# A recurrence's projection and its preparation, put into one stage with the low rank tile first

## The reference

```
h = x @ w_in[l];  p = first 1664 columns of h
p = p + mu * (p_prev - p)                       # p_prev: p one position earlier
r, k, v, wl, al = split(p, 512, 512, 512, 64, 64)
w_log = -softplus(-(w0 + tanh(wl) @ w2)) - 0.5
decay = exp(-exp(w_log));  a = sigmoid(a0 + al @ a2)
kk = k * k_k, each head of 64 divided by its norm
k = k * (1 + (a - 1) * k_a)
step t:  S = S * decay + (S @ -kk) (kk * a)^T + v k^T;   y = S @ r
y = group norm of y + sum(r * k * r_k) * v
```

## Time and profile before

| | us |
|---|---|
| Median of 3 runs | 3826.53 |
| Lowest and highest of them | 3826.25, 3833.31 |
| The profiled execution, its device time | 3837.09 |
| Its span in the profile | 3835.3 |
| PE busy in it | 3369.2 |
| DVE busy | 1380.3 |
| ACT busy | 1086.7 |
| POOL busy | 1404.6 |

### The profile page before, as it was taken

The page is one execution under the profiler, slowest core; times in us unless marked ns, Lnnn a source line. Parts: engine busy times, 40 slices in busy tenths (PEclk is TensorE's granted clock), DMA queues, the critical chain, the costliest instruction groups (busy, mean ns, idle before and its releaser), DMA issues. The chain is left out here.

```text
span 3835.3 us, 52393 instructions
## 1 busy us (share of the span) xinstructions
PE 3369.2 (88%) x20950; PEld 2515.3 (66%) x20950; DVE 1380.3 (36%) x2308; ACT 1086.7 (28%) x1770; POOL 1404.6 (37%) x791
## 2 busy tenths in 40 slices
PE   6688899899967889997999697989999988789998
PEld 5474477566445764775665375678888866467786
DVE  2642463577425424453775322630000032340000
ACT  2313323312023233223211342532212233342221
POOL 4321434522024223344321114734324332655453
PEclk9899899999988999998999898999999989899999
DMA  3001032345210010232443210012111111012232
GB/s 113 7 4 55 29 115 72 121 172 190 88 57 31 3 40 22 94 110 72 186 165 137 76 34 33 9 53 66 61 66 61 62 52 45 23 61 88 85 102 83
DMA packets 75032, 282.17 MB, mean 74 GB/s; under 512 B 8320, under 2 KB 8320, under 8 KB 73888
## 3 DMA queue, kind: packets, MB, share of 16 engines
q1 hardware_dynamic: 74784, 278.76, 21.4%
HBM read 276.62 MB, written 2.10 MB: 73 GB/s over the span
## 5 line engine op out<-in xcount | busy, mean ns | idle before, releaser
L129 POOL TENSOR_TENSOR lows<-ring,highs 128x1024 fp32r<-128x1024 f32 x328 | 813.8, 2482 | 1733.2 <-ACT highs L121 1733.1
L150 PE MATMUL ps<-x_high,highs 128*128 128x512 f32 x2128 | 861.4, 405 | 138.8 <-POOL lows L129 105.7
L153 PE MATMUL ps<-x_low,highs 128*128 128x512 f32 x2128 | 840.1, 395 | 0.0
L154 PE MATMUL ps<-x_high,lows 128*128 128x512 f32 x2128 | 839.6, 395 | 0.0
L150 PEld LDWEIGHTS ps<-x_high,highs 128*128 128x128 f32 x2128 | 407.2, 191 | 240.5 <-POOL lows L129 121.1
L121 ACT ACTIVATE highs<-ring 128x1024 fp32r<-128x1024 f32 x328 | 346.7, 1058 | 714.0 <-PE ps L150 617.6
L153 PEld LDWEIGHTS ps<-x_low,highs 128*128 128x128 f32 x2128 | 407.6, 192 | 91.2 <-issue 9.3
L154 PEld LDWEIGHTS ps<-x_high,lows 128*128 128x128 f32 x2128 | 406.4, 191 | 87.3
L1405 DVE CUSTOM_DVE_ANT_0 X<-X 128x1024 f32<-128x1024 f32 x192 | 321.7, 1675 | 118.4 <-DMA X<-in_ada 112.4
L1361 PE MATMUL ps<-BR,ring 128*128 128x512 f32 x512 | 236.1, 614 | 27.6 <-POOL BR L1413 16.3
L2196 DVE TENSOR_TENSOR hidden_scratch<-ps,hidden_scratch 128x512 f32<-128x512 f32 x66 | 39.8, 603 | 557.2 <-PE ps L154 555.1
(11 more groups left out here) (359 smaller groups left out, 4965.5 us busy)
## 6 DMA issues: line engine op xcount, KB each, us to landing
ring<-in_w SPq DMA_DIRECT2D x402, 512.0 KB, 3.6
X<-in_ada SPq DMA_DIRECT2D x96, 512.0 KB, 6.6
more_tiles<-in_dft SPq DMA_DIRECT2D x2, 2048.0 KB, 8.3
X<-in_xT SPq DMA_DIRECT2D x4, 512.0 KB, 7.4
X<-in_memT SPq DMA_DIRECT2D x2, 1024.0 KB, 5.0
X<-in_cond SPq DMA_DIRECT2D x4, 512.0 KB, 5.5
out<-xT SPq DMA_DIRECT2D x1, 2048.0 KB, 6.3
cst<-in_cst SPq DMA_DIRECT2D x1, 1408.0 KB, 10.4
```

Source lines behind the costliest of these rows:

```text
L129: nc.gpsimd.tensor_tensor(self.low(n), self.chunk(n), self.high(n).bitcast(F32), ALU.subtract).then_inc(self.lo_made, 1)
L150: mm = nc.tensor.matmul(ps, high, xhigh, start=start, stop=False)
L153: nc.tensor.matmul(ps, high, xlow, start=False, stop=False)
L154: return nc.tensor.matmul(ps, low, xhigh, start=False, stop=stop)
```

## The change

The two stages become one. The chunks of w_in are stored in the order RW_ORDER = (12, 4, 5, 6, 7, 0, 1, 2, 3, 8, 9, 10, 11): low rank tile, k, r, v. Chunk i of this order is tile RW_ORDER[i] and goes to bank i % 4; banks 4 to 7 are for the preparation's matmuls. PE now waits for DVE's mix of chunk i-4 before it reuses the bank, since DVE reads the tile from PSUM as well.

SP sends the first chunk, the parameters, two more chunks, and only then clears the other pool. praw has two slots instead of 13, and the mix takes the unshifted tile from PSUM. The 32 operations that fill AR become 8, each over all 512 positions.

The steps of the preparation stand behind the work of chunk i on each engine:

| engine | behind chunk i |
|---|---|
| PE | 1: w2 products; 2: a2 products; 5: norm sums; 10: bonus sums |
| ACT | 0: tanh; 1 and 2: sigmoids; 3 and 5: decays (4 Exp each); 4: squares; 6: Ln; 7: Exp |
| DVE | 1 to 4: one k * k_k each; 2: scans; 3: k_a scale; 4: new k; 6: bound; 8: kk, kk * a; 9: r * k * r_k; 10 and 11: AR; end: bonus |
| POOL | low parts up to chunk 8, 9, 10, 11, each followed by one k product; chunk 12, then four kk * a products, then the next stage's first low part |

```diff
+RW_ORDER = (12, 4, 5, 6, 7, 0, 1, 2, 3, 8, 9, 10, 11)
...
             def _(sp):
+                stream.send(sp, n0 + 1)
+                sp.dma_start(par[:, :], A["par1"][bass.ds(layer, 1), :, :].rearrange("l p c -> p (l c)")).then_inc(S("par"), 16)
+                stream.send(sp, n0 + RING)
                 clear(sp, other)
+                stream.send(sp, n0 + RW_TILES + RING - 1)
+                sp.wait_ge(S("par"), 16)
...
             def _(pe):
+                for i in range(RW_TILES):
+                    if i >= 4:
+                        pe.wait_ge(S("mixed"), i - 3)
+                    gemm3(pe, i % 4, n0 + i, XH, XL, S("product"))
+                    if i == 1:
+                        pe.wait_ge(S("tanh"), 1)
+                        for c in range(4):
+                            nc.tensor.matmul(PS[:, 4 + c, :], w2a2[0:64, c * P:(c + 1) * P], TH[0:64, :], start=True, stop=True).then_inc(S("lora"), 1)
+                    if i == 2:
+                        for c in range(4):
+                            pe.wait_ge(S("gates"), c + 1)
+                            nc.tensor.matmul(PS[:, 4 + c, :], w2a2[64:128, c * P:(c + 1) * P], M[64:128, 12, :], start=True, stop=True).then_inc(S("lora"), 1)
+                    if i == 5:
+                        pe.wait_ge(S("gates"), 8)
+                        for c in range(4):
+                            pe.wait_ge(S("ksq"), c + 1)
+                            nc.tensor.matmul(PS[:, 4 + c, :], C("head_ones", P), TMP[:, c, :], start=True, stop=True).then_inc(S("knorm2"), 1)
+                    if i == 10:
+                        for c in range(4):
+                            pe.wait_ge(S("rkr"), c + 1)
+                            pe.wait_ge(S("kfloor"), c + 1)
+                            nc.tensor.matmul(PS[:, 4 + c, :], C("head_ones", P), TMP[:, c, :], start=True, stop=True).then_inc(S("bonus_sum"), 1)
...
+                for n, steps in ((8, ()), (9, (k_tilde, 0)), (10, (k_tilde, 1)), (11, (k_tilde, 2)), (12, (k_tilde, 3)), (13, (b_tilde, 0))):
+                    stream.lo(nc, pool, n0 + n)
+                    if steps:
+                        steps[0](steps[1])
+                for c in range(1, 4):
+                    b_tilde(c)
+                stream.lo(nc, pool, n0 + RW_TILES + 1)
...
+                    a.activation(praw[:, i % 2, 1:T + 1], PS[:, i % 4, :], ACT.Copy).then_inc(S("evicted"), 1)
+                    stream.hi(nc, act, n0 + min(i + 3, RW_TILES + 1))
...
+                for i, t in enumerate(RW_ORDER):
+                    dve.wait_ge(S("evicted"), i + 1)
+                    v.tensor_tensor(diff[:, i % 2, :], praw[:, i % 2, 0:T], PS[:, i % 4, :], ALU.subtract).then_inc(S("diff"), 1)
+                    dve.wait_ge(S("diff"), i + 1)
+                    v.scalar_tensor_tensor(out=M[:, t, :], in0=diff[:, i % 2, :], scalar=par_col("mu", t),
+                                           in1=PS[:, i % 4, :], op0=ALU.mult, op1=ALU.add).then_inc(S("mixed"), 1)
...
+                    if i == 8:
+                        for c in range(4):
+                            dve.wait_ge(S("kinv"), c + 1)
+                            v.tensor_tensor(KK[:, c, :], KK[:, c, :], SG[:, c, :], ALU.mult).then_inc(S("kk"), 1)
+                        for c in range(4):
+                            dve.wait_ge(S("kk"), c + 1)
+                            v.tensor_tensor(AA[:, c, :], AA[:, c, :], KK[:, c, :], ALU.mult).then_inc(S("b0"), 1)
+                    if i == 9:
+                        for c in range(4):
+                            dve.wait_ge(S("mixed"), 6 + c)
+                            dve.wait_ge(S("kmod"), c + 1)
+                            v.scalar_tensor_tensor(out=TMP[:, c, :], in0=M[:, c, :], scalar=par_col("r_k", c), in1=M[:, 4 + c, :],
+                                                   op0=ALU.mult, op1=ALU.mult).then_inc(S("rkr"), 1)
...
-    out = [cols("rw", t) for t in range(13)]
+    out = [cols("rw", t) for t in RW_ORDER]
```

More of the change, by code:

```diff
@@ L502, in first @@
         n0 = FIRST["rwkv"]
-        praw = X[:, 30 * T:30 * T + 13 * 513].rearrange("p (c t) -> p c t", c=13)
         M = XT(0, 13)
[L505 to L545, removed]
         SG, LC = XT(13, 4), XT(17, 4)
@@ L580, in _, with k_tilde @@
             @block.gpsimd
             def _(pool):
-                for c in range(4):
+                def k_tilde(c):
                     pool.wait_ge(S("decays"), 2 * c + 2)
@@ L585, in _, with b_tilde @@
                     nc.gpsimd.tensor_tensor(KT[:, c, :], M[:, 4 + c, :], PI[:, c, :], ALU.mult).then_inc(S("k_tilde"), 1)
+                def b_tilde(c):
                     pool.wait_ge(S("b0"), c + 1)
                     nc.gpsimd.tensor_tensor(BT[:, c, :], AA[:, c, :], PI[:, c, :], ALU.mult).then_inc(S("b_tilde"), 1)
+                for n, steps in ((8, ()), (9, (k_tilde, 0)), (10, (k_tilde, 1)), (11, (k_tilde, 2)), (12, (k_tilde, 3)), (13, (b_tilde, 0))):
[5 more added lines that the diff above has]
+                stream.lo(nc, pool, n0 + RW_TILES + 1)
             @block.scalar
@@ L591, in _ @@
                 a = nc.scalar
[L592 to L609, removed]
@@ L617, in _ @@
                 v = nc.vector
+                v.memset(praw[:, :, 0:1], 0.0).then_inc(S("zeroed"), 1)
                 v.memset(PP[:, :, :, 0:1], 1.0).then_inc(S("first_decay"), 1)
[L619 to L641, removed]
-                    v.scalar_tensor_tensor(out=TMP[:, c, :], in0=M[:, c, :], scalar=par_col("r_k", c), in1=M[:, 4 + c, :],
-                                           op0=ALU.mult, op1=ALU.mult).then_inc(S("rkr"), 1)
@@ L644, in _ @@
[L644 to L659 removed]
+                dve.wait_ge(S("par"), 16)
```

94 lines of the change are left out of this document (76 added, 18 removed).

## The result

The changed kernel takes 3794.4 us (median of 4 runs, 3793.7 to 3796.5), against 3829.9 (3826.3 to 3836.1, 4 runs) for the kernel before on the same chip: a recorded ratio of 0.9897, 95% interval 0.9879 to 0.9914 (the two medians alone give 0.9907). That is faster, by about 1%, but above the forecast of 3772.3 and above its range (3757 to 3788). The profiled execution took 3793.7 us with a span of 3791.9, against 3837.1 and 3835.3 before.

The account below looks back on a forecast made before the run. TensorE bounds most of the kernel, but waits in the preparation on a VectorE/ScalarE chain. Per layer 46.2 + 3.5 - 13.8 - 5.7 - 3.1 = 27.1 us, twice 54.2, from 3826.5 to 3772.3; range 3757 to 3788.

Parts of the forecast that it names:

- the stall at the bonus sums: After tile 10, PE waits 2.0 to 3.2 us per layer for VectorE's r * k * r_k products; taken 2.6.
- the scans: Behind chunk 2, four VectorE scans may hold out GpSimd's low part: PE stalls 0 to 0.9 us, taken 0.5.
- preparation removed: Between the last product and the scan's first matmul, the whole 46.2 us goes, in each of two layers.
- head: At the stage's opening, the first chunk goes out earlier: gain 3.5 us per layer, ends 2.7 and 3.9.
- matmuls among the tiles: Sixteen fp32 matmuls on PE between GEMM tiles, 0.86 us each at full clock: 13.8 us per layer.
- tail: After the last product, eviction, mix, bonus products and boundary remain: 5.7 us per layer, ends 4.9 and 8.
- rival 1: Smooth case: no stalls, short tail, scan opening at full clock; 32.7 us per layer, 3761; chance 0.18.
- ACT's slots: Behind chunks 3, 6 and 7, table load and four functions end by +5.1 or +5.2, under 5.44 us: no cost.
- Starved GpSimd: In the GEMM, closed VectorE bursts hold low parts to their end; PE loses 14 us per layer, 3794; chance 0.13.
- The third: In-order engines hold the added steps until the last tile; only 9.0 us per layer saved, 3809; chance 0.03.
- the fourth: Slower than before: late steps carry from tile to tile, 3 us stall in each, 3844; chance 0.03.
- the forecast's own: Main case across the stage: stalls of 1 to 6 us per layer, 3764 to 3783 us; chance 0.62.

Follow-up runs that it names:

- The run with the constants: Changed kernel plus five fp32 128x512 matmuls on constants on PE behind chunk 10, ahead of the wait for r * k * r_k: 3790.2 us, ratio 0.9880.
- both runs on it: Changed kernel with SyncE's old order (clear, parameters, chunks) put back: 3801.4 us. Kernel before with only the new order: 3831.7 us.
- The fills in place of the products: Changed kernel with GpSimd's eight k_tilde and b_tilde products replaced by memsets: 3788.2 us; the same replacement in the kernel before: 3823.2 us.

## Why the prediction was right or wrong

The direction held, and so did most of the mechanism; the stall at the bonus sums, which left out two causes, did not, and neither did the base. The miss of the median is 3794.4 - 3772.3 = 22.1 us. I split it first:

- 10.8 us: the sum was 54.2, and the profiled executions differ by 43.4. Of this 10.2 lie in the terms below and 0.6 outside the stage.
- 10.6 us: the base. I carried the sum from the profiled execution to a median of three runs that lay 10.6 us lower, as if that distance would stay. The changed kernel's median is within 1 us of its profiled execution. In three later sets of runs, on three chips, the kernel before had medians of 3837.7 (7 runs), 3838.4 (15) and 3834.5 (13), 8 to 12 above the 3826.5. So the three runs may be a low draw, or their chip may be a faster one; no run tells which.
- 0.7 us: the rest, the median of 3794.4 against the profiled 3793.7.

Either of the first two alone would have left the time inside the range (3772.3 + 10.8 = 3783.1).

The sum, term by term, for both layers. The forecast's stall term of 3.1 per layer is 0.5 for the scans and 2.6 for the bonus sums.

| term | forecast | measured | difference in gain |
|---|---|---|---|
| preparation removed | 92.4 | 92.3 | -0.1 |
| head | 7.0 | 7.8 | +0.8 |
| matmuls among the tiles | 27.6 | 29.3 | -1.7 |
| tail | 11.4 | 12.9 | -1.5 |
| stalls | 6.2 | 13.9 | -7.7 |

**The stall at the bonus sums** is the step that failed. The place (after tile 10), the engine that ends it and the operand were as forecast. The size was not: I had 2.0 to 3.2 us, and it was 6.4 and 7.5 beyond the sums' 3.44. Two things were wrong in it. First, I let VectorE's eight products meet GpSimd's low parts alone: one to wait for until +4.0 and one of 2.3 us in the row or behind it. The row took 11.2 us instead of 4.9, and the timelines of the changed kernel show four operations of GpSimd beside it, two low parts and two k products:

```profile
93.84 2.39 POOL L130 TENSOR_TENSOR lows<-ring,highs 128x1024 fp32r<-128x1024 f32 x1 [1.78 <-ACT highs L122]
94.23 5.45 DVE L656 TENSOR_TENSOR X<-X 128x512 f32<-128x512 f32 x4
96.19 1.74 POOL L556 TENSOR_TENSOR BR<-X 128x512 f32<-128x512 f32 x1
99.28 2.66 POOL L130 TENSOR_TENSOR lows<-ring,highs 128x1024 fp32r<-128x1024 f32 x1 [1.35 <-ACT highs L122]
99.60 5.77 DVE L659 TENSOR_TENSOR X<-X 128x512 f32<-128x512 f32 x4
101.90 1.72 POOL L556 TENSOR_TENSOR BR<-X 128x512 f32<-128x512 f32 x1
```

In my list of the slots GpSimd's k products had no place, although the change's table has one behind each of these low parts. Their part is shown by two experiments that take them away in different ways: both give a row of 9.0 us and a wait of PE of 2.24 us in both layers, 2.2 less. That is inside the 2.0 to 3.2 that I had, so the wait was priced rightly but for the k products. (The +9.9 of the working should read +8.9, 4.0 + 4.9; with the low part's 2.3, the mix's 1.5 and a first product of 0.7 that is 13.4, inside its 13 to 14, so the slip moved nothing.) That the low parts hold the rest follows from the rows, but no run took those away. Second, I priced the idle time at its length alone. PE left it at a lower clock, 0.65 over the sums of layer 0, and slot 10 was 2.0 and 3.1 us longer than the wait and the sums explain. The run with the constants took 1.7 and 2.8 of that back by keeping PE busy; 0.3 stays unassigned. I had written of a clock lost in the tail, in rival 1, and did not apply it to a wait between tiles.

**The head** was 3.9 per layer, the upper end that I gave, and both runs on it (5.0 and 3.9 lost, 3.8 and 2.9 gained) agree as far as openings of 14.3 to 16.2 us let one tell.

**The matmuls**: the norm sums are 3.44, as taken. The groups behind tiles 1 and 2, the ones on 64 rows, lengthened their slots by 3.89 and 3.90, 0.45 each over that price. Their row is 3.70 for eight instructions, so the rest lies around them. I did not try what it is.

**The tail** was 6.4 against 5.7. The fills in place of the products bring it to 5.0, so GpSimd's share is 1.4 us where I had 0.5. AR itself was late as feared: its operation of L672 at 122.72 took 2.85 us instead of 0.68, and mix 12 began at 126.09, 1.7 us after its eviction's end.

**What I costed at nothing.** ACT's slots held: after a table load of 1.28 us the next activation follows at once, and the four Exp end before the next eviction:

```profile
62.06 1.05 ACT L122 ACTIVATE highs<-ring 128x1024 fp32r<-128x1024 f32 x1
63.13 1.28 ACT L577 ACT_TABLE_LOAD   x1
64.43 0.64 ACT L577 ACTIVATE X<-X 128x512 f32<-128x512 f32 x1
```

The Trainium skill, ScalarE: Activation LUTs, What ACT_TABLE_LOAD costs, adds 1.38 us of drain to each switch. The trace does not show one, as before, and no slot ran over. The scans (0.5 forecast) cost PE nothing: GpSimd did get in between them, and their row of four took 6.72 us instead of 4.9, but the low part took 2.92 and came in time:

```profile
54.77 6.72 DVE L637 TENSOR_TENSOR_SCAN X<-cst,X 128x512 f32<-128x512 f32 x4
57.49 2.92 POOL L130 TENSOR_TENSOR lows<-ring,highs 128x1024 fp32r<-128x1024 f32 x1 [6.93 <-ACT highs L122]
```

**The rivals.** Smooth (3761) is out: there was a stall, and the scan opened slow (33 instructions in 2.15 us, where the earlier trace rows has 61 in 1.91 at full clock; the whole group of 64 took 3.69, as before). Starved GpSimd (3794) has the right number by another road. PE never waited for a low part inside the GEMM, and its stall came from VectorE, so that rival fell. The third and the fourth are out by the windows. The case that happened is the forecast's own, with a stall beyond its 1 to 6 us per layer.

The rule that I set beside the second rival, from the Trainium skill, SBUF — State Buffer, Who interferes with whom, is that whoever starts first has the shared ports for the whole instruction. The rows agree for single instructions. What the rule leaves open is what made the difference here: with both engines queued, the rows show either a strict change of turns (the 11.2 us) or one engine shut out for a whole row (the 9.3 us).

## What to carry to other kernels

When steps are moved under a bound engine, list for every slot all the instructions of VectorE and GpSimd that read two SBUF tiles, the ones that the change brings included, and add them up as if on one engine. Price a wait of PE as its length plus the slower matmuls behind it. And take the base of a forecast from the same kind of execution as the sum: the median of three here lay 8 to 12 us below those of the three later sets.

## What the runs showed of the hardware that I had not expected

- VectorE's scans also share with GpSimd: four took 6.72 us with a low part between them, and 4.9 alone.
- VectorE's operations with one input in PSUM do not: mixes with GpSimd beside them took 0.68 and 0.75 us, and GpSimd's low part fell from 2.74 to 2.39 us when the mix began to read PSUM.
- Removing VectorE's work can return little: AR in 8 instead of 32 operations took 4.8 us instead of 11.7 in layer 0 and 6.5 in layer 1, and gave 3.0 and 1.6. GpSimd was held out until the row's end in both layers (7.67 us for one product), and it ended last, not VectorE.
- Of two waits of the same 2.24 us in one execution, one left the clock at 1.00, and behind the other it averaged 0.67. With fills in place of the products, both sums behind such a wait were slow (5.39 and 5.40 us). What PE did before was the same row of tiles in all four. Why they differ stays open.
